# Sixteen pairs of feed-forward chunks computed with seven block products in place of eight

## The reference

```python
D_MODEL, SEQ, D_FF = 1024, 256, 2816

def swiglu(h, w_in, w_out):
    gate, up = jnp.split(h @ w_in, 2, axis=-1)      # w_in: (1024, 5632)
    return (jax.nn.silu(gate) * up) @ w_out         # w_out: (2816, 1024)

x = x + 0.5 * swiglu(rmsnorm(x, norm_g[layer, 0]), ffn_w_in[layer, 0], ffn_w_out[layer, 0])
```

## Time and profile before

| what | value |
|---|---|
| times of three runs | 2125.14, 2126.56, 2126.80 us (median 2126.56) |
| span of the profiled execution | 2123.9 us |
| PE busy | 2075.8 us, 98% |
| PE weight loads busy | 1744.1 us, 82% |
| DVE busy | 1196.0 us, 56% |
| ACT busy | 1031.3 us, 49% |
| POOL busy | 71.6 us, 3% |
| moved by DMA | 359.98 MB, 169 GB/s over the span |

### The profile page before, as it was taken

The page is one execution under the profiler, slowest core; times in us unless marked ns, Lnnn a source line. Parts: engine busy times, 40 slices in busy tenths (PEclk is TensorE's granted clock), DMA queues, the critical chain, the costliest instruction groups (busy, mean ns, idle before and its releaser), DMA issues.

```text
span 2123.9 us, 26075 instructions
## 1 busy us (share of the span) xinstructions
PE 2075.8 (98%) x10491; PEld 1744.1 (82%) x10491; DVE 1196.0 (56%) x1542; ACT 1031.3 (49%) x1359; POOL 71.6 (3%) x113
## 2 busy tenths in 40 slices
PE   8999999999999999999999999999999999989999
PEld 6887988888888878888888889888888787877887
DVE  5545687555645576654565446655555555765454
ACT  6435436444544468644454444544455444764443
POOL 2000000000000000000000000007001000000000
PEclk9999999999999999999999999999999999989999
DMA  8553425655555442565555544586647654114553
GB/s 260 191 195 120 159 91 173 212 179 191 175 196 193 140 159 80 178 218 179 178 178 180 197 158 159 188 244 195 179 138 173 204 191 168 62 57 162 178 180 117
DMA packets 259880, 359.98 MB, mean 169 GB/s; under 512 B 19582, under 2 KB 200234, under 8 KB 259760
## 3 DMA queue, kind: packets, MB, share of 16 engines
q1 hardware_dynamic: 256800, 351.57, 50.4%
q0 software_dynamic: 2016, 4.95, 1.5%
q10 hardware_dynamic: 944, 1.79, 0.3%
HBM read 356.70 MB, written 1.57 MB: 169 GB/s over the span
## 4 chain that ended last, share of the span: by engine, by line
PE 87%; DVE 6%; ACT 4%; issue 1%; DMA 1%; ACTq 0%; DVEq 0%; SPq 0%
PE bank L421 17%; PE bank L423 16%; PE bank L422 16%; PE acc L718 6%; PE acc L720 6%; PE acc L719 6%; PE bank L416 2%; PE bank L417 2%; PE bank L418 2%; PE tr L699 2%; DVE w_lo_ L445 2%; ACT w_hi_ L435 1%; PE acc L748 1%; PE acc L750 1%; PE acc L749 1%
## 5 line engine op out<-in xcount | busy, mean ns | idle before, releaser
L445 DVE TENSOR_TENSOR w_lo_<-raw_in,w_hi_ 128x2048 fp32r<-128x2048 f32 (+1 forms) x333 | 574.1, 1732 | 214.0 <-ACT w_hi_ L435 213.7
L421 PE MATMUL bank<-w_hi_,xt_hi_ 128*128 128x512 f32 x1648 | 658.4, 400 | 2.6 <-DVE xt_lo_ L545 2.4
L423 PE MATMUL bank<-w_hi_,xt_lo_ 128*128 128x512 f32 x1648 | 643.6, 391 | 0.0
L422 PE MATMUL bank<-w_lo_,xt_hi_ 128*128 128x512 f32 x1648 | 642.4, 390 | 0.0
L435 ACT ACTIVATE w_hi_<-raw_in 128x2048 fp32r<-128x2048 f32 (+1 forms) x333 | 481.7, 1461 | 64.7 <-DMA raw_in<-ffn_w_in 31.3
L844 DVE TENSOR_TENSOR wo_lo_<-raw_out,wo_hi_ 128x2048 fp32r<-128x2048 f32 x80 | 183.8, 2297 | 484.2 <-ACT wo_hi_ L798 484.2
L423 PEld LDWEIGHTS bank<-w_hi_,xt_lo_ 128*128 128x128 f32 x1648 | 309.4, 188 | 66.3
L421 PEld LDWEIGHTS bank<-w_hi_,xt_hi_ 128*128 128x128 f32 x1648 | 310.0, 188 | 64.9 <-issue 4.8
L422 PEld LDWEIGHTS bank<-w_lo_,xt_hi_ 128*128 128x128 f32 x1648 | 310.2, 188 | 59.0
L798 ACT ACTIVATE wo_hi_<-raw_out 128x2048 fp32r<-128x2048 f32 x80 | 153.3, 1916 | 369.7 <-PE acc L720 359.3
L718 PE MATMUL acc<-wo_hi_,ht_hi_ 128*128 128x512 f32 x576 | 224.3, 389 | 2.7 <-DVE ht_lo_ L831 2.7
(11 more groups left out here) (379 smaller groups left out, 2088.0 us busy)
## 6 DMA issues: line engine op xcount, KB each, us to landing
raw_in<-ffn_w_in SPq DMA_DIRECT2D x352, 512.0 KB, 4.9
raw_out<-ffn_w_out SPq DMA_DIRECT2D x88, 1024.0 KB, 5.0
raw_in<-hg_w_in SPq DMA_DIRECT2D x16, 1024.0 KB, 5.2
raw_in<-fox_w_in SPq DMA_DIRECT2D x16, 1024.0 KB, 5.4
raw_in<-conv_w_in SPq DMA_DIRECT2D x12, 1024.0 KB, 5.1
raw_in<-hg_w_out SPq DMA_DIRECT2D x4, 1024.0 KB, 5.0
raw_in<-fox_w_out SPq DMA_DIRECT2D x4, 1024.0 KB, 5.2
raw_in<-conv_w_out SPq DMA_DIRECT2D x4, 1024.0 KB, 5.0
```

Source lines behind the costliest of these rows:

```text
L421: mm(o, xt_hi[:, k, tok], wh[:, par, k, 0:w], start=first, stop=False)
L422: mm(o, xt_hi[:, k, tok], wl[:, par, k, 0:w], start=False, stop=False)
L423: last = mm(o, xt_lo[:, k, tok], wh[:, par, k, 0:w], start=False, stop=end)
L445: dve.e.tensor_tensor(g.piece(g.wl, n, half, k), raw, g.piece(g.wh, n, half, k).bitcast(F32), ALU.subtract).then_inc(g.w_lo, 4 if k is Non ...
```

## The change

In six of the eight feed-forward stages some neighbouring chunks are computed in pairs: chunks (2,3), (5,6) and (8,9) in stages 1 to 4, and (4,5) and (7,8) in stages 0 and 7. Stages 5 and 6 stay as they were. That makes 16 pairs.

For a pair, the product of the tokens and the weights is seen as 2x2 blocks. On the token side the blocks are token tile by half of the features (A11, A12, A21, A22). On the weight side they are half of the features by gate or up columns of both chunks (B11, B12, B21, B22), each 4 k-tiles of 512 columns, 1 MB. Eight block products are replaced by seven (Winograd's form). With T3 = B12+B22, T2 = B11+T3, T4 = B21+T2 and T1 = T2-B22, and S1 to S4 the matching sums of the A blocks, PE multiplies A11 by B11, A12 by B21, S2 by T2, S3 by T3, S1 by T1, S4 by B22 and A22 by T4, each 4 k-tiles x 3 matmuls (`pe_pair`). The sums of weights are 128x2048 DVE additions in place (`dve_block_sum`), except for T3: POOL issues a DMA that loads B22 again and adds it to B12 in SBUF. The four S blocks (128x512) are added and split once in each stage. Seven DVE instructions of 128x512 put the products together, and silu and the multiplication by `up` run over 512 columns at once.

The weight blocks land in four tiles of the arena, apart from `raw_in`, and the ring of split weights is now counted in halves (`OPN`, `USED`). SP loads the four blocks of the next pair while a pair runs. In stage 7 the first pair is at chunk 4, and its blocks are loaded at chunks 1 and 2. The masks of the recurrence mixer are loaded by POOL after the last pair of stage 0 and not at the start, since a combined block uses their place; the two small loads of the attention mixer and its memset come one stage later.

The core of the diff:

```diff
+PAIRED = {f: (2, 5, 8) if f in (1, 2, 3, 4) else (4, 7) for f in (0, 1, 2, 3, 4, 7)}
+PAIRS = [(f, c) for f in range(8) for c in PAIRED.get(f, ())]
...
+B11, B21, T2, T3, T1, B22, T4 = range(7)
...
-        self.wh = sb("w_hi_", [P, 2, KT, CW], F32R)
+        self.wh = sb("w_hi_", [P, 4, KT // 2, CW], F32R)
...
+            op = OPN[N0[S_FFN[PAIRS[p - 1][0]]] + PAIRS[p - 1][1]]
+            sp.wait_ge(g.w_lo, 4 * (op + (T1, T3, T4, B22)[i]) + 4)
+            sp.wait_ge(g.st_add, 3 * p)
+        sp.e.dma_start(g.blocks[i], v[:, i // 2 * 4:i // 2 * 4 + 4, i % 2, c * FC:(c + 2) * FC]).then_inc(
+            (g.b11_in, g.b12_in, g.b21_in, g.b22_in)[i], 16)
...
+                if form == "S":
+                    while todo < c:
+                        w_out_chunk(todo)
+                        todo += 1
+                    if next_pair_early(p):
+                        for which in (0, 1, 3, 2):
+                            block(p + 1, which)
+                    w_out_chunk(c)
+                    todo = c + 1
+                    p += 1
+                    continue
+                i += 1
+                if before == "S":
+                    chunk(i)
+                    w_out_chunk(c - 1)
+                    todo = c
+                    continue
...
+def pe_pair(g, pe, f, p, turn, second, q, pending):
+    s, c = S_FFN[f], PAIRS[p][1]
+    n, u, j = N0[S_FFN[f]] + c, U[S_FFN[f]], list(PAIRED).index(f)
+    x = lambda half, t: tuple(v[:, 4 * half:4 * half + 4, t * P:(t + 1) * P] for v in (g.xt_hi_, g.xt_lo_))
+    a, y, z = g.bank[0], g.bank[1], g.tr[1]
+    def product(bank, of_x, i):
...
+    pe.wait_ge(g.xt_lo, 16 * u + 16)
+    pe.wait_ge(g.st_c, 7 * p)
+    product(z, x(0, 0), B11)
+    pe.wait_ge(g.h, 22 * f + 2 * q + 2)
+    product(y, x(1, 0), B21)
+    turn(q)
+    if c == PAIRED[f][0]:
+        second(pending)
+    product(a, summed(A_S2), T2)
+    if c != PAIRED[f][0]:
+        second(pending)
+    pe.wait_ge(g.st_c, 7 * p + 1)
+    product(y, summed(A_S3), T3)
+    pe.wait_ge(g.st_cp, p + 1)
+    product(z, summed(A_S1), T1)
+    pe.wait_ge(g.st_c, 7 * p + 2)
+    product(a, summed(A_S4), B22)
+    pe.wait_ge(g.st_c, 7 * p + 3)
+    product(z, x(1, 1), T4)
+    second(q)
...
+    elif i == T3:
+        wait_t3(g, act, p)
+    else:
+        act.wait_ge(g.st_add, 3 * p + {T2: 1, T4: 2, T1: 3}[i])
+    act.wait_ge(g.prod, USED[op - 4])
+    act.e.activation(g.wh[:, op % 4], g.block_of(i), ACT.Copy).then_inc(g.w_hi, 4)
...
+    elif i == T2:
+        wait_t3(g, dve, p)
+        dve.wait_ge(g.w_lo, 4 * (op + B11) + 4)
+        dve.e.tensor_tensor(b11, b11, b12, ALU.add).then_inc(g.st_add, 1)
+    elif i == T4:
+        dve.wait_ge(g.w_lo, 4 * (op + B21) + 4)
+        dve.wait_ge(g.st_add, 3 * p + 1)
+        dve.e.tensor_tensor(b21, b21, b11, ALU.add).then_inc(g.st_add, 1)
+    else:
+        dve.wait_ge(g.b22_in, 16 * (p + 1))
+        dve.wait_ge(g.w_lo, 4 * (op + T2) + 4)
+        dve.wait_ge(g.st_add, 3 * p + 2)
+        dve.e.tensor_tensor(b11, b11, b22, ALU.subtract).then_inc(g.st_add, 1)
...
+            pool.wait_ge(g.b12_in, 16 * (p + 1))
+            pool.e.dma_start(g.blocks[1], w[:, KT // 2:, 1, c * FC:(c + 2) * FC], accum_op=ALU.add).then_inc(g.t3_in, 16)
...
+    def pair(p, q, pending):
+        c, n = PAIRS[p][1], N0[s] + PAIRS[p][1]
+        act_block(g, act, p, T2)
+        if c != PAIRED[f][0]:
+            turn(pending)
+            weights_out(pending)
+            act_block(g, act, p, T3)
+        act.wait_ge(g.prod, PDN[n] + 1)
+        if p:
+            act.wait_ge(g.silu, 22 * PAIRS[p - 1][0] + 2 * PAIRS[p - 1][1] + 4)
+        act.e.activation(g.p1s, g.tr[1][:], ACT.Copy).then_inc(g.st_cp, 1)
+        if c == PAIRED[f][0]:
+            act_block(g, act, p, T3)
+        act_block(g, act, p, T1)
+        act.wait_ge(g.st_c, 7 * p + 1)
+        act.wait_ge(g.rstd, 2 * R[s] + 1)
+        act.e.activation(g.silu0, g.silu0, ACT.Silu, scale=g.rstd_[:, 0:1]).then_inc(g.silu, 2)
+        act_block(g, act, p, B22)
+        act_block(g, act, p, T4)
+        turn(q)
+        weights_out(q)
+        act_split(g, act, n + 2, 0)
+        act_split(g, act, n + 2, 1)
+        if c + 3 in PAIRED[f]:
+            act_block(g, act, p + 1, B11)
+        act.wait_ge(g.st_c, 7 * p + 7)
+        act.wait_ge(g.h, 22 * f + 2 * q + 2)
+        act.wait_ge(g.squares, 4 * R[s] + 4)
+        act.wait_ge(g.rstd, 2 * R[s] + 2)
+        act.e.activation(g.sq[:], g.p1s, ACT.Silu, scale=g.rstd_[:, 1:2]).then_inc(g.silu, 2)
...
+    def pair(p, q, pending):
+        c, n, first_one = PAIRS[p][1], N0[s] + PAIRS[p][1], PAIRS[p][1] == PAIRED[f][0]
+        a, y, z = g.bank[0], g.bank[1], g.tr[1]
+        def gate0():
+            dve.wait_ge(g.prod, PDN[n] + 2)
+            dve.wait_ge(g.st_cp, p + 1)
+            dve.wait_ge(g.h, 22 * f + 2 * q + 2)
+            dve.e.tensor_tensor(g.silu0, y[:], g.p1s, ALU.add).then_inc(g.st_c, 1)
+        dve_block(g, dve, p, T2)
+        if first_one:
+            dve_block(g, dve, p, T3)
+            dve_block_sum(g, dve, p, T1)
+            gate0()
+            dve_x_sum(g, dve, f, A_S3)
+            dve_x_sum(g, dve, f, A_S1)
+        else:
+            dve_block_sum(g, dve, p, T1)
+            turn(pending)
+            weights_out(pending)
+            dve_block(g, dve, p, T3)
+            gate0()
+        dve_block(g, dve, p, T1)
+        if first_one:
+            dve_x_sum(g, dve, f, A_S4)
+        dve.wait_ge(g.prod, PDN[n] + 3)
+        dve.wait_ge(g.st_c, 7 * p + 1)
+        dve.e.tensor_tensor(g.p1s, a[:], g.p1s, ALU.add).then_inc(g.st_c, 1)
+        dve_block(g, dve, p, B22)
+        if not first_one:
+            dve_block(g, dve, p, T4)
+            turn(q)
+            weights_out(q)
+        dve.wait_ge(g.prod, PDN[n] + 5)
+        dve.wait_ge(g.st_c, 7 * p + 2)
+        dve.wait_ge(g.h_turned, 12 * f + (0 if first_one else PAIRS[p - 1][1] + 2))
+        dve.e.tensor_tensor(g.up0, z[:], g.p1s, ALU.add).then_inc(g.st_c, 1)
+        if first_one:
+            dve_block(g, dve, p, T4)
+            turn(q)
+            weights_out(q)
+        dve_split(g, dve, n + 2, 0)
+        dve.wait_ge(g.st_c, 7 * p + 3)
+        dve.e.scalar_tensor_tensor(g.up1, y[:], -1.0, g.up0, ALU.mult, ALU.subtract).then_inc(g.st_c, 1)
+        dve.e.tensor_tensor(g.p1s, y[:], g.p1s, ALU.add).then_inc(g.st_c, 1)
+        dve_split(g, dve, n + 2, 1)
+        dve.wait_ge(g.prod, PDN[n] + 6)
+        dve.wait_ge(g.st_c, 7 * p + 4)
+        dve.e.scalar_tensor_tensor(g.up0, a[:], -1.0, g.up0, ALU.mult, ALU.subtract).then_inc(g.st_c, 1)
+        dve.wait_ge(g.silu, 22 * f + 2 * c + 2)
+        dve.wait_ge(g.st_c, 7 * p + 6)
+        dve.wait_ge(g.rstd, 2 * R[s] + 2)
+        dve.e.scalar_tensor_tensor(g.up0, g.up0, g.rstd_[:, 0:1], g.silu0, ALU.mult, ALU.mult).then_inc(g.h, 2)
+        dve.wait_ge(g.prod, PDN[n] + 7)
+        dve.e.tensor_tensor(g.p1s, z[:], g.p1s, ALU.add).then_inc(g.st_c, 1)
+        dve.wait_ge(g.silu, 22 * f + 2 * c + 4)
+        dve.e.scalar_tensor_tensor(g.up1, g.up1, g.rstd_[:, 1:2], g.sq[:], ALU.mult, ALU.mult).then_inc(g.h, 2)
...
+                dve_x_sum(g, dve, f, A_S2)
+                if f != 7:
+                    dve_block(g, dve, p, B11)
+                weights_out(c - 1)
+                read(0)
+                turn(c - 1)
+                if f == 7:
+                    dve_block(g, dve, p, B11)
+                dve_block(g, dve, p, B21)
+                read(1)
+                dve_block_sum(g, dve, p, T3)
+                dve_block_sum(g, dve, p, T2)
+                dve_block_sum(g, dve, p, T4)
+            else:
+                dve_block(g, dve, p, B11)
+                if before == "S":
+                    weights_out(c - 2)
+                    turn(c - 2)
+                else:
+                    turn(pending)
+                    weights_out(pending)
+                read(0)
+                dve_block_sum(g, dve, p, T3)
+                dve_block_sum(g, dve, p, T2)
+                dve_block(g, dve, p, B21)
+                read(1)
+                dve_block_sum(g, dve, p, T4)
```

466 lines of the change are left out of this document (375 added, 91 removed).

## The result

The changed kernel takes 2109.67 us (median of 4, 2109.03 to 2110.07) against 2126.35 (2125.14 to 2126.80): ratio 0.9924, 95% interval 0.991 to 0.9938. It is faster, by 16.7 us where 32.6 were forecast, and 0.7 us above the top of the range. The profiled span went from 2123.9 to 2108.8 us, 15.1 less.

What follows compares the result with a forecast made beforehand. PE was taken as the bound, busy for 2075.8 of 2123.9 us. The span was to be 2123.9 - 43.5 + 10.6 = 2091.0 us, and the median, 2.7 above it, 2094 us, with a range of 2084 to 2109.

Steps and rivals of the forecast that it cites:

- The 43.5 us: On PE, 192 matmuls of 128x512 fewer over 16 pairs, at 0.2267 us each, were to save 43.5 us.
- The first pairs: DVE's gapless 21.6 us chain makes PE wait: 1.6 us in each of five stages, 2.6 in stage 7, 10.6 together.
- Edits that I cost at nothing: S-block additions and copies, first pairs' block loads at 324 GB/s, and moved mask and small loads were to cost nothing.
- The adding DMA ... is hidden: POOL's load-and-add for T3 lands in 11 to 15 us, may take up to 23, and so costs nothing.
- The four additions run where DVE waits: At a stage's start, S-block additions (2.8 us on DVE) are covered by DVE's 2.45 us wait for ACT.
- The new products have the same shape, so I take the same price: On PE, the pairs' products step at 0.2267 us per matmul, like the old ones.
- 0.24 us: Sign against the forecast: a pitch of PE's product matmuls (L839) above this.
- The later pairs lose nothing: In the 10 later pairs DVE's results reach PE in time; the tightest margin, `ht_lo_` before a turn, is 2.5 us.
- DVE or the loads run a little late: Rival, chance 0.18: DVE steps of 2.29 us in first pairs give 2101; with `raw_out` late in 10 pairs too, 2109.

Runs made afterwards that it cites:

- version 15: Changed kernel with the edits of 12, the arena first in memory, and stage 7's additions on x moved to chunk 1: 2089.42 us, ratio 0.9828.
- run 5: Changed kernel with all splits of x sums early and, in first pairs, VectorE summing T1 before splitting T3 and splitting T4 earlier: 2102.19 us.
- run 11: Changed kernel with the arena, and `sums_split` in it, as the first buffer in memory: 2107.01 us, ratio 0.9909.
- Run 4: Changed kernel with VectorE splitting all four sums of x together in the plain chunk ahead of the first pair: 2109.39 us, ratio 0.9919.
- run 2: Changed kernel with the first pair's adding DMA in stages 0 and 7 held until chunk 3's `raw_in` has landed: 2104.65 us, ratio 0.9899.
- run 1: Changed kernel without the pairs of stages 0 and 7, so 12 pairs in stages 1 to 4 alone: 2107.62 us, ratio 0.9913.
- 6: Changed kernel with output weights split ahead of copying the turned hidden tile in a stage's last plain chunk behind a pair: 2111.99 us, ratio 0.9933.
- 12: Changed kernel with the edits of run 2 and run 5 together: 2095.96 us, ratio 0.9860.
- 13: Same as 12, with the four additions on x made in chunk 1 instead of chunk 0 in stages 0 and 7: 2098.16 us, ratio 0.9870.
- run 7: Changed kernel loading only half of the last chunk's output weights in the six paired stages (output not the reference's): 2108.06 us, ratio 0.9908.
- run 14: The changed kernel measured and profiled again, unchanged: 2111.08 us, ratio 0.9927.
- run 9: Changed kernel with `sums_split` laid out in strides, its four sums inside each k: 2110.22 us, ratio 0.9928.

## Why the prediction was wrong

Measured by its own sum, the span should have been 2123.9 - 43.5 + 10.6 = 2091.0 and was 2108.8.

*The 43.5 us* held as the price of what was removed. In version 15 two stages get every bit of it.

*The first pairs* (10.6) were right in place and near in size, not in mechanism. PE's two visible stalls in stage 1 are 0.52 and 0.58 us above the step. From turn to turn a first pair costs more than that, and the starts of PE's `turn` (L888) say what it is made of (us from the turn in the pair to the next one):

| interval | changed | run 5, new order | run 11, arena first | run 15 |
|---|---|---|---|---|
| first pair, stages 0 to 4 | 32.20 | 30.76 | 32.20 | 30.39 |
| first pair, stage 7 | 33.09 | 31.09 | 33.10 | 31.11 |
| second pair | 30.75 | 30.75 | 30.40 | 30.40 |
| third pair | 25.31 | 25.31 | 24.95 | 24.96 |

The order gives back 1.44 us in each of five stages and 2.0 in stage 7. The place of `sums_split` gives 0.35 in a later pair and nothing in a first one; only when the order is right too does a first pair gain by it, 0.37. So without the pitch the first pairs cost some 9.5 us (5 x 1.44, and 2.3 in stage 7) for my 10.6. It is not the sum of VectorE's work that was late, as the step said, but a loop: VectorE's sum, ScalarE's copy, VectorE's split. Run 4 took 2 us out of the chain and won nothing.

*"Edits that I cost at nothing"* is the step that failed first. I gave the blocks of a first pair 324 GB/s and asked only whether they were in time for the pair. I laid out the loads of a steady period, with the adding DMA in it, and did not do so for chunks 1 to 3 of stages 0 and 7, where four 1 MB blocks and the adding DMA join the chunks' own loads. I never asked what else was in that queue. The price is 6.4 us by the stages of run 2 (5.3 against the second profile of the changed kernel), 5 by the medians.

*"The adding DMA ... is hidden"* held by itself: landing 12.3 to 14.9 us where 11 to 15 were given, median 14.3, and VectorE's sums did not wait for it. What failed is that I priced it only by its own landing. It took bandwidth from its neighbours, which moved 74 GB/s beside it and 364 without it. On the Trainium skill's rule (SBUF — State Buffer, Who interferes with whom) that such splits do not keep GpSimd from its descriptors, the trace agrees: L1042 took 1.27 to 1.36 us each of 16 times, with a VectorE instruction running beside it every time.

*"The four additions run where DVE waits"* was right in stages 1 to 4 (to turn 0 within 0.02 us) and wrong in 0 and 7, 0.77 and 0.45 us. The cover was read from stage 2 alone.

*"The new products have the same shape, so I take the same price"* missed 0.005 to 0.008 us a matmul: 0.35 us in each of ten later pairs and 0.37 in each of six first ones, 5.7 us in all by the table above. Nothing in the profile of before could tell it, for it hung on where the new buffer lay. I had set 0.24 us as the pitch that would refute me, and it was 0.233: too coarse a mark, as 768 matmuls multiply it.

*"The later pairs lose nothing"* held for the waits I named in the changed kernel; in seven other runs (1, 5, 6, 11, 12, 13 and 15) the tightest of them, `ht_lo_` ahead of a turn, came up in a second pair, with 0.2 to 0.9 us. What I did not lay out is the stage's last unit: in a paired stage PE runs `second` later beside the last chunk, so the last output weights are issued and land too late, 0.5 to 1.4 us in six stages, 4.6 in all (run 7).

Together, from turn to turn: 6.5 us for the late loads in chunk 3 of stages 0 and 7 (2.35 and 4.20, of which some 1.3 in stage 7 did not come again in run 14), 5.7 for the pitch, 4.7 for the ends and 1.2 for the additions make 18.1. The first pairs without the pitch cost 1.1 less than I had. The slower clock in the mixer ahead of stage 3 is 1.7, the other mixers and the part behind stage 7 are 0.9, and stage 6 gave back 1.7 by chance. That makes 2091.0 + 18.1 - 1.1 + 1.7 + 0.9 - 1.7 = 2108.9, and the span was 2108.8. What is open is why the clock fell behind that wait and what the 0.5 us behind stage 7 are.

Of the rivals, "DVE or the loads run a little late" gave the right time (2109) by luck: loads were late, but in chunk 3 of two stages and at six ends, not in the ten later pairs, and VectorE's steps did not cost the full 2.29 (two of them take from 389.39 to 393.80, 2.2 each). The chances as listed add up to 0.93 for faster and 0.05 for slower, where the last line says 0.92 and 0.06.

## What to carry to other kernels

When an edit adds loads, lay out the DMA queue for every stretch in which they run, above all the irregular one at the start, and ask who else waits on it. Price a new kind of transfer by what it does to its neighbours, not by its landing. If a chain on one engine is "gapless", look for the hand-over to another engine inside it before taking work out: order can be worth more than work. And when the saving is in hundreds of matmuls, compare the step of the new ones with the old to 0.001 us.

## What the runs showed of the hardware

- With an adding DMA of 1 MB in flight the 16 DMA engines, as busy as before, moved 229 GB/s, 155 of it the adding DMA's, and 364 in the same stretch without it. Over the changed kernel's page a byte on GpSimd's queue took 1.9 times the engine time of one on SyncE's. The adding DMA landed in 12.3 to 14.9 us.
- The step of a 128x512 matmul depended on where the buffers lie in memory: with `sums_split` as the stationary operand 0.2323 to 0.2352 us on average at one place and 0.2271 to 0.2277 at another. It did not depend on its layout or its values. The weight load's own duration, 188 ns, shows nothing of it.
- After a stall of PE of 1.8 to 2.8 us in a feed-forward stage, or of 3.1 to 3.9 us in the mixer ahead of stage 3, some matmuls sometimes ran at the lower clock (0.43 us a step, 1.6 us in all for eight of them), and sometimes not. In stage 7 a stall of 2.32 us was followed by it in the first profile of the changed kernel, and one of 2.58 in run 14 was not; in the mixer one of 3.14 us was in run 9 and was not in run 1.
